# Half of a scan's decay products, moved from VectorE to GpSimd, in a two-layer hybrid trunk

## What is computed

```python
def ssd_scan(xs, dt, a, bm, cm, h0):
    ...
    a_cum = jnp.cumsum((dt * a).reshape(b, nc, q, SSD_GROUPS, SSD_HPG), axis=2)
    ...
    decay = jnp.exp(jnp.where(lower[:, :, None, None], seg, NEG_INF))
    cb = jnp.einsum("bclgn,bcsgn->bclsg", cc, bc)
    y_diag = jnp.einsum("bclsgr,bcsgrp->bclgrp", cb[..., None] * decay, xdt)
    decay_to_end = jnp.exp(a_cum[:, :, -1:] - a_cum)
    states = jnp.einsum("bcsgn,bcsgrp->bcgrpn", bc, xdt * decay_to_end[..., None])
    ...
```

## Time and profile before

| | |
|---|---|
| median of 3 runs | 1251.89 us (1251.78 to 1254.09) |
| the profiled execution: its own time | 1253.19 us |
| its span | 1251.3 us, mean granted clock 0.998 |
| PE busy | 1191.4 us (95% of the span) |
| DVE busy | 826.8 us (66%) |
| ACT busy | 572.0 us (46%) |
| POOL busy | 85.5 us (7%), 73 instructions |

### The profile page before, as it was taken

One profiled execution on the slowest core, in us unless ns is written; L12 is line 12 of the kernel. 1 busy time (PEld: TensorE's weight loads), 2 busy tenths in 40 slices (PEclk: granted clock), 3 DMA queues, 4 the chain that ended last, 5 costly groups with the idle time before them and its releaser, 6 DMA issues.

```text
span 1251.3 us, 17140 instructions
## 1 busy us (share of the span) xinstructions
PE 1191.4 (95%) x6392; PEld 940.9 (75%) x6392; DVE 826.8 (66%) x1205; ACT 572.0 (46%) x982; POOL 85.5 (7%) x73
## 2 busy tenths in 40 slices
PE   5999899898987999999999999999999899999998
PEld 3567677676766787787887887886887568988997
DVE  3663697897967563785585684785665985745655
ACT  3531374736557423632331421424744674744543
POOL 0000102010020024000000000044000003000000
PEclk9999999999999999999999999999999999999999
DMA  9667243241421234354544543542243004455554
GB/s 359 251 254 281 84 123 113 72 131 51 144 76 60 84 101 156 135 185 135 181 159 146 195 140 134 202 150 67 96 141 117 17 2 135 148 180 190 188 186 151
DMA packets 46684, 179.02 MB, mean 143 GB/s; under 512 B 5088, under 2 KB 7456, under 8 KB 43552
## 3 DMA queue, kind: packets, MB, share of 16 engines
q1 hardware_dynamic: 46336, 177.66, 41.1%
q10 hardware_dynamic: 288, 0.56, 0.1%
HBM read 177.05 MB, written 1.15 MB: 142 GB/s over the span
## 4 chain that ended last, share of the span: by engine, by line
PE 72%; DVE 16%; ACT 6%; issue 3%; DMA 2%; DVEq 0%; SPq 0%; ACTq 0%
PE ps L1709 48%; PE ps L1716 8%; PE ps L1971 6%; DVE cacc L1408 4%; PE ps L1799 1%; ACT ey L1121 1%; PE ps L1732 1%; DVE sm L1657 1%; DVE ey L1484 1%; ACT u L1019 1%; DVE mixF L1510 1%; DVE xbc L1421 1%; DVE w_lo L1258 1%; DVE ycomb L1495 1%; DVE prob L1682 1%
## 5 line engine op out<-in xcount | busy, mean ns | idle before, releaser
L967 ACT ACTIVATE w_hi<-raw 128x1024 fp32r<-128x1024 f32 x206 | 216.7, 1052 | 243.3 <-DMA raw<-in_w_ff 179.4
L1258 DVE TENSOR_TENSOR w_lo<-raw,w_hi 128x1024 fp32r<-128x1024 f32 x206 | 256.8, 1247 | 98.2 <-ACT w_hi L967 98.0
L1709 PE MATMUL ps<-a_hi,w_hi 128*128 128x512 f32 (+1 forms) x868 | 318.4, 367 | 0.4 <-DVE w_lo L1258 0.4
L1709 PE MATMUL ps<-a_hi,w_lo 128*128 128x512 f32 (+1 forms) x868 | 307.6, 354 | 0.0
L1709 PE MATMUL ps<-a_lo,w_hi 128*128 128x512 f32 (+1 forms) x868 | 307.4, 354 | 0.0
L1709 PEld LDWEIGHTS ps<-a_hi,w_hi 128*128 128x128 f32 x868 | 164.1, 189 | 27.5 <-issue 2.6
L1709 PEld LDWEIGHTS ps<-a_lo,w_hi 128*128 128x128 f32 x868 | 164.2, 189 | 25.0 <-issue 1.0
L1709 PEld LDWEIGHTS ps<-a_hi,w_lo 128*128 128x128 f32 x868 | 164.0, 189 | 23.2
L1709 PE MATMUL ps<-b_hi,w_hi 128*128 128x512 f32 x304 | 119.2, 392 | 0.0
L1709 PE MATMUL ps<-b_lo,w_hi 128*128 128x512 f32 x304 | 118.4, 390 | 0.0
L1709 PE MATMUL ps<-b_hi,w_lo 128*128 128x512 f32 x304 | 118.3, 389 | 0.0
(11 more groups left out here) (257 smaller groups left out, 1656.5 us busy)
## 6 DMA issues: line engine op xcount, KB each, us to landing
raw<-in_w_ff SPq DMA_DIRECT2D x128, 512.0 KB, 3.4
mring<-in_w_mod SPq DMA_DIRECT2D x24, 1024.0 KB, 6.9
mring<-in_w_mod SPq DMA_DIRECT2D x32, 768.0 KB, 5.0
raw<-in_w_in_even SPq DMA_DIRECT2D x36, 512.0 KB, 5.7
ey<-acum_rows SPq DMA_DIRECT2D x32, 384.0 KB, 4.8
raw<-in_w_in_odd SPq DMA_DIRECT2D x18, 512.0 KB, 3.5
raw<-in_w_out_even SPq DMA_DIRECT2D x16, 512.0 KB, 3.4
raw<-in_w_out_odd SPq DMA_DIRECT2D x8, 512.0 KB, 3.8
```

The source lines that it names most:

```text
L967: nc.scalar.activation(w_hi[:, u % RING, :, :], raw[:, u % RING, :, :], ACT.Copy).then_inc(hi_done, 1)
L1258: v.tensor_tensor(w_lo[:, u % RING, :, :], raw[:, u % RING, :, :], w_hi[:, u % RING, :, :].bitcast(F32), ALU.subtract).then_inc(lo_done, 1)
L1709: ins = mm(out_ap, w_[:, n % RING, k, :], (x_[k][:, 0:ntok] if type(x_) is list else x_[:, k, 0:ntok]), start=(k == 0 and j == 0), stop=(k ...
```

## The change

The products of the backward direction (16 of the 32) leave DVE and go to POOL, at the same places of the step list. A new semaphore `gb_done` counts them. PE waits for both counts before `y`, and DVE waits for the backward products of the group before when it overwrites `cbm`. A helper gives POOL the semaphore that says that `cbm` is written.

```diff
+        def freed_of(key):
+
+            what, n = freed_by[key]
             return signalled(what), n
...
+                elif st[0] == "seg" and st[2] == "b":
+                    n = seg_n[st]
+                    if n % (2 * NCH) == 1:
+                        pool.wait_ge(*freed_of(("cb", st[1])))
+                    pool.wait_ge(seg_done, n + 1)
+                    ey = decay_tile(n // 2)[:, 1, :, :]
+                    pool.tensor_tensor(ey, ey, cbm[:, st[3], 1, None, :].broadcast_to([P, R, P]), ALU.mult).then_inc(gb_done, 1)
                 elif st[0] == "state":
...
                     dve.wait_ge(*filled(st))
                     dve.wait_ge(*latest())
+                    if st[1]:
+                        dve.wait_ge(gb_done, NCH * st[1])
...
                 elif k == "seg":
                     di = dirs[st[2]]
+                    if di:
+                        continue
                     dve.wait_ge(seg_done, seg_n[st] + 1)
...
-                    pe.wait_ge(g_done, 2 * n + 2)
+                    pe.wait_ge(g_done, n + 1)
+                    pe.wait_ge(gb_done, n + 1)
```

More of the change, by code:

```diff
@@ L639, in trunk @@
         rows_in = [[sem(f"rows_in{i}{d}") for d in "fb"] for i in range(3)]
-        names = ("arow_done rows_out grow_done htok_done unit_done sines_done hv_done mfull_done dtrow_done acc_sq tmp_sq mu_used row_done mcol_done modc_done sil_done hi_done lo_done c0_in dft_in xsq_done xrms_done xr_done xn_done xnt_done xu_done c1_in vec_in wdt_in bias_in dve_seq act_seq consts_set vt_done "
+        names = ("gb_done arow_done rows_out grow_done htok_done unit_done sines_done hv_done mfull_done dtrow_done acc_sq tmp_sq mu_used row_done mcol_done modc_done sil_done hi_done lo_done c0_in dft_in xsq_done xrms_done xr_done xn_done xnt_done xu_done c1_in vec_in wdt_in bias_in dve_seq act_seq consts_set vt_done "
                  "silc_done th0_done h_done sq_done var_done rstd_done nt_done u_done split_done coef_done "
@@ L649, in trunk @@
         S = {n: sem(n) for n in names}
-        (arow_done, rows_out, grow_done, htok_done, unit_done, sines_done, hv_done, mfull_done, dtrow_done, acc_sq, tmp_sq, mu_used, row_done, mcol_done, modc_done, sil_done, hi_done, lo_done, c0_in, dft_in, xsq_done, xrms_done, xr_done, xn_done, xnt_done, xu_done, c1_in, vec_in, wdt_in, bias_in, dve_seq, act_seq,
+        (gb_done, arow_done, rows_out, grow_done, htok_done, unit_done, sines_done, hv_done, mfull_done, dtrow_done, acc_sq, tmp_sq, mu_used, row_done, mcol_done, modc_done, sil_done, hi_done, lo_done, c0_in, dft_in, xsq_done, xrms_done, xr_done, xn_done, xnt_done, xu_done, c1_in, vec_in, wdt_in, bias_in, dve_seq, act_seq,
          consts_set, vt_done, silc_done, th0_done, h_done, sq_done, var_done, rstd_done, nt_done,
@@ L670, in emptied @@
             what, n = free_before[key]
+            return signalled(what), n
+        def freed_of(key):
+            what, n = freed_by[key]
             return signalled(what), n
```

## The result

| | before | changed |
|---|---|---|
| median | 1251.99 us (1251.78 to 1254.09, 4 runs) | 1280.71 us (1278.85 to 1283.07, 4 runs) |
| ratio, 95% interval | | 1.0226 (1.0206 to 1.0246) |
| span of the profiled execution | 1251.3 us | 1281.2 us (its own time 1283.07) |
| POOL busy | 85.5 us | 110.3 us |

The change makes the kernel slower, as forecast, but by 28.7 us (28.3 by the ratio, 1.0226 times 1252) and not by 21.3. The time lies 1.7 us above the range, in the place of the rival "both delays add up" (1279). In what follows the lines of the changed file lie 12 to 17 further down: L967 is the old L955, L1907 the old L1891, L1934 the old L1918, L1898 the old L1882, L1417 and L1420 the old L1405 and L1408, L1270 the old L1258, L1500 DVE's product, and L956 the new product on POOL.

What follows compares the result with a forecast made beforehand. PE's matmuls bound the kernel, waiting in the scan on DVE. Groups' 5.0 + 4.5 + 4.5 + 6.0 plus 1.3 for the clock gave 21.3 us, so 1251.9 + 21.3 = 1273.2 us, range 1264 to 1279.

Steps and rivals of the forecast that it cites:

- both delays add up: Rival: slow clock stretches slot 1 and the exponentials, DVE waits every round and pays hits too; some 27 us, 1279; chance 0.12.
- The product's price: One 128 x 768 backward product on POOL: 1.84 us, with 1.66 and 1.94 as the ends.
- The hold: POOL's fourth to sixth scalings queue behind each group's first backward product; slot 1 late by 3.9, 7.7, 7.7, 6.9 us.
- PE gets back at most its 5.3: Second and third group: being late, PE regains at most 5.3 us of waits for DVE; its own bound is +2.4.
- DVE's bound in a middle group: Second and third group: late states +2.4, three products fewer -2.9, three hits by POOL +5.0, so +4.5 us each.
- The clock: PE's slow clock after its new wait before the fourth state: 1.3 us in the last group, none in the others.
- The first group, +5.0: First group of the scan: DVE's bound +4.1 us, plus 0.9 for waiting on ACT's late forward exponential.
- The last group, +6.0 and 1.3 for the clock: Last group: PE's hold of 6.9 less a vanished 0.92 us wait; later products hidden in DVE's waits; clock 1.3 extra.
- the signs that I had named for being wrong: L1408 keeping 0.76 us beside a product, fourth state not waiting for the first product, or new PE waits for `gb_done`.
- Some 5 us of cover: PE's `gb_done` wait before `y`: the later backward products are asked for a slot after they are made.
- DVE loses nothing to POOL: Rival: POOL and DVE overlap, or POOL runs in DVE's pauses; PE's bound counts, 1264 to 1270, say 1267; chance 0.17.
- faster: Rival: DVE's relief decides if the states are not held and no hit is paid; 12.6 us gained, 1239; chance 0.03.

Runs made afterwards that it cites:

- warm: The changed kernel plus filler matmuls on PE before each group's fourth state (3 in the first group, 8 in the others), results never read: 1274.62 us, ratio 1.0164.
- wait_only: The kernel before, all products on DVE, but POOL waits for the first backward product's exponential between third and fourth scaling: 1269.87 us, ratio 1.0117.
- b0_only: The changed kernel with only each group's first backward product on POOL, at its place; the other 12 back on DVE: 1275.55 us, ratio 1.0162.
- b0_warm: b0_only plus filler matmuls on PE before the fourth state (3 in the first group, 8 in the others): 1270.62 us, ratio 1.014.
- b123_only: The changed kernel with each group's first backward product back on DVE; the other 12 stay on POOL: 1257.52 us, ratio 1.0026.
- b123_none: b123_only with its 12 products on POOL left out on both engines, so the output lacks them: 1247.24 us, ratio 0.9947.
- behind: The changed kernel with each group's first backward product moved behind all six states, still on POOL: 1249.09 us, ratio 0.9949.

## Why the prediction was right and wrong, step by step

**The product's price: right.** 1.84 us taken, 1.80 to 1.85 measured, 2.29 at most where it waits for DVE.

**The hold: right in its place and size, wrong in the wait that it makes.** The fourth scaling was to end 13.3 us behind the start of `ysum` (226.5 - 213.19); it ended at 13.3 (235.53 - 222.22). The sixth state was to come 7.7 us later than before (7.6 by the summands; the first group's 3.9 is 3.8): in warm, at full clock, it is 7.6 later, and in the changed kernel 8.7. But PE's wait is 8.6 us and not "about 6" or "some 7": the third state of before ends 4.8 us behind the sum, and 13.3 less 4.8 is 8.5 by the forecast's own numbers. wait_only and b0_only show that this hold, not the offload as such, is the loss.

**"PE gets back at most its 5.3": only a bound, and DVE's own bound was the one to use.** The wait for the next group's tile did not go (3.6 us to 4.7), as DVE, later itself, sets it.

**DVE's bound in a middle group, "+2.4 - 2.9 + 5.0 = +4.5": right without the slow clock.** In warm, whose clock is full there, the group is 4.5 us longer than before (78.67 - 74.15). Its parts: the first L1417 starts 18.56 us behind the sum (239.23 - 220.67) against 15.47, so +3.1, of which I had 2.4; three hits, as foreseen, but of 1.5 us and not 1.65, so +4.5. The two errors cancel.

**"The clock. ... I take 1.3 us in the last group, where PE leads, and none in the others, where DVE's bound is later by 2.1": this is the step that failed.** I took DVE's bound as one that PE's clock cannot move. But DVE waits for PE's states and, behind slot 1, for ACT's exponential. In the changed kernel's second group the first L1417 starts 18.88 us behind the sum (+3.4) and the forward product waits 1.60 us: +3.4 + 1.6 - 2.9 + 4.6 = +6.7, and measured is +6.5 (80.64 - 74.15). The clock's whole price by the comparison with fillers is 1.5 us in the first group, 2.0 and 1.0 in the middle ones and 2.6 in the last: 7.1 us by the groups and 7.8 by the medians, where I had 1.3. I had even priced one half of it, 0.9 us for the first group's exponential, and not carried the same chain to the others. The stretch at half clock was also longer than the one of before that I had read (6.1 us twice and 3.9 once, behind a wait of 8.6, against some 3 behind one of 4.2). But the main miss was who waits behind it.

**The first group, +5.0: measured +6.4.** Without the slow clock b0 alone gives +3.8 (b0_warm), and b1 to b3 give +1.1 (b123_only, counted from the fourth state), 4.9 in all, as forecast. The clock's 1.5 us make it 6.4.

**The last group, +6.0 and 1.3 for the clock: +5.9 and 2.6.** b123_only has +0.1 there: the products b1 to b3 are hidden in it, as foreseen, though not without a trace: the 2.3 us wait for `gb_done` is one of the signs that I had named for being wrong. "Some 5 us of cover" does not hold at that place.

**Sum.** Without the clock I had 20.0 us; warm gives 20.5 by the medians and 19.9 by the groups, without the 1.6 us before the first group's states. With the clock's 7 to 8 in place of 1.3 the sum would have been 27 to 28, and the measured value is 28.3 by the ratio. The likeliest case should have been the one that I called "both delays add up". Its time, 1279, is near, but not all of its working: in the middle groups DVE waits for the exponential in the first round and not in every one, and the hits are smaller than I had taken and not larger.

**The rival "DVE loses nothing to POOL" is out** by b123_only against b123_none and by the stretched L1420. **The rival "faster"** had its condition right, that b0 must not hold the states, and its price wrong: with the hold gone and the hits paid, "behind" gains 6.4 us; but moving the step alone gains 7.9, so no part of the gain is shown to come from POOL.

## What to carry to other kernels

Before work goes to an idle engine, look at what stands behind it in that engine's queue: here the wait for ACT alone, on an engine with nothing to do, cost 14.6 us, more than the work that was moved, and putting the step three places later gained 7.9 us where no offload gained anything. A stall that you add to TensorE has to be counted with the slow clock that follows it (here 7 to 8 us for four stalls), and followed through ACT and VectorE into the next round, even where TensorE is not the later of two bounds. And a GpSimd instruction that reads SBUF did not run in parallel to the VectorE instructions with two tensor inputs there: what VectorE is relieved of (0.96 us a product) comes back as a hit (1.5 us).

## What the runs showed of the hardware that was not expected

I had expected only DVE's instructions with two tensor inputs in SBUF to be held up. In "behind", b0 falls on a L1417, with one tensor input and two columns of factors. POOL:

```profile
224.76 1.85 POOL L956 TENSOR_TENSOR ey<-ey,cbm 128x768 f32<-128x768 f32 x1 [4.47 <-ACT ey L1136]
```

and DVE:

```profile
225.18 1.72 DVE L1417 TENSOR_SCALAR cacc<-cpad,vec 128x512 f32<-128x512 f32 x1
226.93 3.11 DVE L1420 SCALAR_TENSOR_TENSOR cacc<-cpad,vec,cacc 128x512 f32<-128x512 f32 x4
```

It takes 1.72 us in place of 0.55, and 1.82 in another place of the same kernel. It ends 0.29 us behind POOL's end (226.90 against 226.61), so it waited through nearly all of the product. The Trainium skill (SBUF — State Buffer, "Who interferes with whom") lists `tensor_scalar` among the operations that can use the shared pair of ports; the row agrees, and no row shows which mode the instruction was in.

Not everything waits: in the last group of "behind" DVE's `hent<-hent,ps` (L1484), whose second input lies in PSUM, starts at 369.70 and takes its usual 0.55 us within POOL's product of 2.09 us from 369.29.

A hit on one of four L1420 costs 1.46 to 1.55 us for a product of 1.84, so 0.3 to 0.4 less than the product, where the 1.29 us rows of before had given 0.2 less; the full 1.84 that the prediction names beside its sum is not reached. A L1270 loses the 1.65 us taken.
